# Loads, matmuls and top-k rounds put in another order at the start of a one-core hybrid decoder step

## What is computed

```python
def index_topk(iq, iw, ik, q_pos, topk):
    s = jax.nn.relu(jnp.einsum('bqhd,bld->bqhl', iq, ik))
    score = jnp.einsum('bqhl,bqh->bql', s, iw).astype(jnp.float32)
    ...
    score = jnp.where(causal, score, -jnp.inf)
    _, idx = lax.top_k(score, topk)
...
    p = rmsnorm(x, norm_mix_g) @ w_in
    a_q, a_k, a_v, i_q, i_k, i_w, p_b, c_q, gates = split_last(p, IN_SIZES)
    a_q = rope_partial(a_q.reshape(B, T, N_HEADS_A, HEAD_DIM_A), pos, ROT_A)
...
    ik_past = cache_idx_k[page_table].reshape(DB, PAST_LEN, IDX_DIM)
```

## Time and profile before

| | |
|---|---|
| median of three runs | 1349.66 us (1349.17 to 1350.88) |
| the profiled execution | 1349.81 us, its span from the first to the last instruction 1347.9 us |
| PE busy | 1234.8 us, 92% of the span |
| DVE busy | 710.7 us, 53% |
| ACT busy | 407.2 us, 30% |
| the p loop's first matmul | at 156.79 us |
| the decode attention's first matmul (L1126) | at 283.42 us |
| mean granted clock of PE | 0.970 |

### The profile page before, as it was taken

One profiled execution on the slowest core, in us unless ns is written; L12 is line 12 of the kernel. 1 busy time (PEld: TensorE's weight loads), 2 busy tenths in 40 slices (PEclk: granted clock), 3 DMA queues, 4 the chain that ended last, 5 costly groups with the idle time before them and its releaser, 6 DMA issues.

```text
span 1347.9 us, 25134 instructions
## 1 busy us (share of the span) xinstructions
PE 1234.8 (92%) x10585; PEld 1094.1 (81%) x10589; DVE 710.7 (53%) x1126; ACT 407.2 (30%) x791; POOL 86.3 (6%) x140
## 2 busy tenths in 40 slices
PE   6699699889969988998998999999999999999995
PEld 4476476658657777887887889999999999999994
DVE  5499798714043284365346337755544434434445
ACT  2110144424322423343234234233333123123120
POOL 0100100002102042002001002000000000000000
PEclk9899799999989999999999999999999999999997
DMA  7113143513500022022013215562122312223211
GB/s 305 31 28 156 35 167 120 178 35 156 200 0 10 33 79 89 18 97 97 18 56 118 73 43 161 170 235 95 63 94 74 114 63 95 95 67 121 77 50 67
DMA packets 39218, 127.52 MB, mean 95 GB/s; under 512 B 5203, under 2 KB 17491, under 8 KB 29635
## 3 DMA queue, kind: packets, MB, share of 16 engines
q1 hardware_dynamic: 37666, 121.36, 25.3%
q0 software_dynamic: 1440, 4.56, 1.0%
HBM read 111.77 MB, written 14.13 MB: 93 GB/s over the span
## 4 chain that ended last, share of the span: by engine, by line
PE 78%; DVE 15%; ACT 2%; issue 2%; DMA 1%; POOL 1%; SPq 0%; DVEq 0%; ACTq 0%; POOLq 0%
PE ps L923 13%; PE ps L924 12%; PE ps L927 12%; PE ps L951 8%; PE ps L1281 4%; PE ps L960 3%; PE ps L961 3%; PE ps L962 3%; PE ps L904 2%; DVE R L1999 2%; DVE small L1998 2%; PE ps L1233 2%; PE ps L946 1%; PE ps L949 1%; DVE wl L558 1%
## 5 line engine op out<-in xcount | busy, mean ns | idle before, releaser
L548 ACT ACTIVATE wh<-land 128x1024 fp32r<-128x1024 f32 (+1 forms) x120 | 116.2, 970 | 185.6 <-PE ps L927 185.6
L951 PE MATMUL ps<-xn,ring 128*128 128x272 f32 x576 | 149.4, 403 | 9.4 <-ACT pb L1593 9.4
L558 DVE TENSOR_TENSOR wl<-land,wh 128x1024 fp32r<-128x1024 f32 (+1 forms) x120 | 136.0, 1136 | 27.7 <-ACT wh L548 26.9
L923 PE MATMUL ps<-xhi,wh 128*128 128x272 f32 x512 | 138.9, 289 | 2.3 <-DVE wl L558 1.2
L923 PE MATMUL ps<-hh,wh 128*128 128x272 f32 x512 | 138.8, 288 | 0.0
L924 PE MATMUL ps<-hl,wh 128*128 128x272 f32 x512 | 138.3, 288 | 0.0
L924 PE MATMUL ps<-xlo,wh 128*128 128x272 f32 x512 | 138.3, 288 | 0.0
L951 PEld LDWEIGHTS ps<-xn,ring 128*128 128x128 f32 x576 | 105.4, 192 | 34.6 <-ACT pb L1593 9.8
L960 PE MATMUL ps<-xhi,wh 128*128 128x272 f32 x384 | 124.2, 324 | 4.2 <-issue 3.6
L961 PE MATMUL ps<-xlo,wh 128*128 128x272 f32 x384 | 113.3, 295 | 0.0
L962 PE MATMUL ps<-xhi,wl 128*128 128x272 f32 x384 | 113.2, 295 | 0.0
(11 more groups left out here) (407 smaller groups left out, 2368.8 us busy)
## 6 DMA issues: line engine op xcount, KB each, us to landing
land<-in_slabs SPq DMA_DIRECT2D x48, 1024.0 KB, 4.8
ring<-in_slabs SPq DMA_DIRECT2D x17, 1024.0 KB, 8.1
gates<-R SPq DMA_DIRECT2D x24, 272.0 KB, 2.0
merge<-gates SPq DMA_DIRECT2D x24, 272.0 KB, 4.1
land<-in_slabs SPq DMA_DIRECT2D x12, 512.0 KB, 3.9
xT<-in_mks SPq DMA_DIRECT2D x8, 512.0 KB, 4.9
R<-in_kv SPq DMA_DIRECT2D x24, 128.0 KB, 2.0
pb<-in_kv SPq DMA_DIRECT2D x24, 128.0 KB, 2.0
```

The costliest lines, as they stand in the source:

```text
L548: act.activation(hi, src, ACT.Copy).then_inc(s["weights_hi"], 1)
L558: eng.tensor_tensor(lo, src, hi.bitcast(F32), ALU.subtract).then_inc(s["weights_lo"], 1)
L923: pe.matmul(ps[:, b + h, 0:HALF], whi[:, k], hi[k][:, c], start=a, stop=False)
L951: mm = pe.matmul(ps[:, b, 0:HALF], W[:, k, c0_:c0_ + w], xn3[:, k, cols], start=a, stop=z)
```

## The change

It touches the kernel up to the decode attention, on every engine.

- **Loads**: the small vectors and the first quarter of x first, then slab 0, the other quarters of x, the constants, slab 1. The order from there on is as before; the key page row `kv_row(0)` is issued after `kv_row(1)`, since its place in SBUF (the start of `xT`) now holds scores of block 3.
- **Head weights**: `iw` had 4 columns. It now has 32, and job 1 puts four of its eight k tiles in each accumulation, each into 32 output partitions of its own (L1007 of the changed kernel). A matmul with the constant `sel` adds the four groups (L1029), in place of a transpose.
- **Prompt scores**: block 3 gets a buffer of its own (`rl3`), and the three blocks are computed early, with pieces of jobs 4 and 5 between them.
- **DVE**: blocks 1 and 2 first, with the rotations of two `aq` tiles after block 1; then the heads' weighing of the decode scores, the norm of the memory and the copies; block 3 last, with the other rotations between its rounds.
- **PE**: jobs 4 to 6, then the decode scores and the memory's norm, then jobs 7 to 9.
- **Fill steps**: 24 steps (three `mk` jobs) go ahead of the p loop (`("pre", 0)`), and from u = 13 on a group has 3 steps in place of 4.
- The memory's norm sums go to PSUM bank 7. The semaphores are renamed: `padded` for `zi_set` and `za_set`, `tables` for `consts` and `bias_done`, `selected` counts `ss_out` too.

```diff
-    s = [("w_in", 0, KT, [(IK, 64), (IK, 64), (IK + 64, 4)]), ("w_in", 0, KT, [(IQ, 256)])]
+    s = [("w_in", 0, KT, [(IK, 64), (IK, 64), (IK + 64, 32)]), ("w_in", 0, KT, [(IQ, 256)])]
...
-    waits = [(("p", u), 5 if u < 13 else 4) for u in range(36)]
+    waits = [(("pre", 0), 24)]
+    waits += [(("p", u), 5 if u < 13 else 3) for u in range(36)]
...
-        rl = cut(R, B + 5312, 4, 512)
+        rl, rl3 = cut(R, B + 5312, 4, 512), cut(xT, 0, 4, 512)
...
-            sp.dma_start(cst[:, 0:first], i["const"][:, 0:first]).then_inc(s["ones_in"], 16)
-            for n in range(2):
-                sp.dma_start(xT3[:, 4 * n:4 * n + 4], i["xT"][:, 4 * n:4 * n + 4]).then_inc(s[f"x_in{n}"], 16)
-            sp.dma_start(vec[:, :], i["vec"]).then_inc(s["ones_in"], 16)
+            sp.dma_start(vec[:, :], i["vec"]).then_inc(s["vec_in"], 16)
...
+            x_pair(0)
...
-            stream(0, 2)
+            stream(0, 1)
+            for n in range(1, 4):
+                x_pair(n)
+            sp.dma_start(cst[:, 0:first], i["const"][:, 0:first]).then_inc(s["ones_in"], 16)
+            stream(1, 2)
...
             sp.wait_ge(s["norm_out"], 8)
-            kv_row(0)
             kv_row(1)
             sp.wait_ge(s["isum"], 12)
+            kv_row(0)
             kv_row(2)
...
+            slab_wait(pe, JOBS[1][2])
+            W, b = slab(0), bank_of(1)
+            for h in range(2):
+                for k in range(KT):
+                    g = slice(32 * (k % 4), 32 * (k % 4) + 32)
+                    mm = pe.matmul(ps[g, b + h, 0:HALF], W[:, k, P:P + 32], xg3[:, k, h * HALF:(h + 1) * HALF],
+                                   start=(k < 4), stop=(k >= 4))
+            mm.then_inc(s["gemm_done"], 1)
...
+            rope(4)
+            part(6, xn3, 2, KT)
+
+            pe.wait_ge(s["padded"], 5)
+            pe.wait_ge(s["rope_sin"], 5)
             for q in range(2):
                 pe.wait_ge(s[f"ki_in{q}"], 128 * 4)
-            pe.wait_ge(s["relu"], 12)
             for b in range(DB):
...
+            norm(1, NMEM)
             pe.wait_ge(s["selected"], 1)
...
-            pe.wait_ge(s["ss_out"], 1)
-            for n in range(3, 8):
-                rope(n)
-
-            pe.wait_ge(s["rope_sin"], 8)
+            part(7, xn3, 0, KT)
+            pe.wait_ge(s["selected"], 2)
+            pe.wait_ge(s["norm_rt"], 2)
+            rope(5)
+            part(8, xn3, 0, 2)
+            rope(6)
+            part(8, xn3, 2, KT)
+            part(9, xn3, 0, 2)
+            rope(7)
+            part(9, xn3, 2, KT)
...
+            pe.wait_ge(s["norm_out"], 16)
+            fill("pre", 0)
...
+            for t in range(1, 3):
+                row_scores(t)
                 for _ in range(TOPK_P // 8):
-                    take_eight(sc, m8)
...
+                    take_eight(scp[:, 0:P * (t + 1)], m8)
+                row_bias(t)
+                if t == 1:
+                    rope(3)
+                    rope(4)
...
             dve.wait_ge(s["ki_used"], 8)
             dve.tensor_scalar(rs, flat, 0.0, iws, ALU.max, ALU.mult).then_inc(s["selected"], 1)
+            norm(1, memT, memn, NMEM, "norm_mem_g")
             dve.wait_ge(s["i_rows"], 2)
...
+            row_scores(3)
+            for n in range(TOPK_P // 8):
+                if n in (6, 10):
+                    rope(5 if n == 6 else 6)
+                take_eight(scp, m8)
+            row_bias(3)
+            rope(7)
```

More of the change, by code:

```diff
@@ L992, in _, with part, prompt_scores @@
                 job(0, xg3, only=k)
-            pe.wait_ge(s["ones_in"], 32)
+            pe.wait_ge(s["ones_in"], 16)
             norm_sum(0)
[L995 to L1001, removed]
-                rope(n)
[L1003 to L1011, removed]
+            slab_wait(pe, JOBS[1][2])
[6 more added lines that the diff above has]
+            mm.then_inc(s["gemm_done"], 1)
+            def part(n, src, first, last):
+                for k in range(first, last):
+                    job(n, src, only=k)
+            def prompt_scores(t):
                 for h in range(4):
@@ L1017, in _ @@
                               start=True, stop=True).then_inc(s["iscore"], 1)
[L1018 to L1022, removed]
+            job(2, xg3)
+            part(3, xg3, 0, 3)
+            pe.wait_ge(s["inputs_in"], 16)
+            out_of(1, pe)
+            for t in range(5):
+                w = P if t < 4 else NS
+                mm = pe.matmul(ps[0:w, 7, 4 * t:4 * t + 4], iwT[:, P * t:P * t + w], k_("sel")[:, 0:4], start=True, stop=True)
+            mm.then_inc(s["i_rows"], 1)
+            rope(0)
+            part(3, xg3, 3, 6)
+            pe.wait_ge(s["padded"], 1)
+            rope(1)
+            part(3, xg3, 6, KT)
+            rope(2)
+            pe.wait_ge(s["rope_out"], 3)
+            prompt_scores(1)
+            part(4, xn3, 0, 2)
+            prompt_scores(2)
+            part(4, xn3, 2, 5)
+            prompt_scores(3)
+            part(4, xn3, 5, KT)
+            part(5, xn3, 0, 5)
+            pe.wait_ge(s["relu"], 12)
+            rope(3)
+            part(5, xn3, 5, KT)
+            part(6, xn3, 0, 2)
+            rope(4)
+            part(6, xn3, 2, KT)
+            pe.wait_ge(s["padded"], 5)
+            pe.wait_ge(s["rope_sin"], 5)
             for q in range(2):
                 pe.wait_ge(s[f"ki_in{q}"], 128 * 4)
-            pe.wait_ge(s["relu"], 12)
             for b in range(DB):
@@ L1551, in norm @@
                 else:
-                    act.activation(nbuf[n][1][:, 0:N], ps[:, 4, 0:N], ACT.Sqrt, bias=epsc, scale=1.0 / D).then_inc(s["norm_rt"], 1)
+                    act.activation(nbuf[n][1][:, 0:N], ps[:, 7, 0:N], ACT.Sqrt, bias=epsc, scale=1.0 / D).then_inc(s["norm_rt"], 1)
             def evac(n):
@@ L1617, in _ @@
             act.wait_ge(s["pool_step"], 2)
+            act.activation(small[:, 142:143], epsc, ACT.Square)
             norm(0, xT3, TOK)
-            act.wait_ge(s["aux_in"], 48)
-            norm(1, memT, NMEM)
-            act.wait_ge(s["norm_out"], 16)
+            act.wait_ge(s["norm_out"], 8)
             for t in range(1, 4):
@@ L1989, in _ @@
                 else:
[L1990 to L1991 removed]
+                    ins.then_inc(s["padded"], 1)
+            dve.tensor_copy(biasp[:, 0, 0:P], k_("caus")).then_inc(s["tables"], 1)
+            rope(0)
+            rope(1)
+            take(3, iq[:, 1])
+            rope(2)
+            dve.wait_ge(s["padded"], 1)
             flat = ps[:, 4:7].rearrange("p a b -> p (a b)")[:, 0:KEYS]
[L1994 removed]
             def take_eight(sc, m8):
@@ L2001, in _, with row_scores @@
             m8 = small[:, 132:140]
-            for t in range(1, 4):
+            def row_scores(t):
                 n = P * (t + 1)
-                sc = scp[:, 0:n]
+                sc, rows = scp[:, 0:n], rl if t < 3 else rl3
                 for h in range(4):
```

113 lines of the change are left out of this document (55 added, 58 removed).

## The result

The change takes 1365.97 us (median of four runs, 1364.68 to 1367.01) against 1349.41 us (1347.54 to 1350.88) for the kernel before: 1.28% slower, ratio 1.0128 with an interval of 1.0109 to 1.0146. Forecast were 1350.3 us, 1346 to 1356. The profiled execution spans 1363.9 us against 1347.9.

What follows compares the result with a forecast made beforehand. It took SP's page reads, then DVE's list, to set the p loop's start: 164.5 + 126.6 - 7.1 = 284.0 us for the decode attention against 283.42, 0.6 us later, so 1350.3 us, range 1346 to 1356.

Steps and rivals of the forecast that it cites:

- What bounds the kernel, and the cover: Front: SP's page reads, 1.25 us each, gate the decode scores, so earlier loads, head weights and prompt scores gain nothing.
- When the pages are there: SP's queue: larger slab 0 adds 0.3 us, last page lands at 101.7 us, PE starts at about 101.8 us.
- The decode scores: On PE after the pause: 15.7 us plus 2.35 us for 4.7 us at half clock, ending at 119.85 us.
- Rival 2: Decode scores on PE: 64-row matmuls don't raise the clock, all run at half, 13.4 us more, 1363.7 us; chance 0.09.
- DVE's list: DVE between decode scores and p loop: norm, copies, block 3, rotations, 44.6 us; p loop starts at 164.5 us.
- PE's own list: PE between decode scores and p loop: norm, sum, jobs, rotations, transposes, fill steps, some 43.5 us, just shorter than DVE's.
- The p loop: Loop before decode attention: fill steps moved ahead shorten it by 7.1 us from 126.6; starting at full clock counted as 0.
- Rivals 3 and 4: P loop: second groups give nothing, 3.7 us more, 1354.0 us, chance 0.13; all steps come back, 1346.6 us, chance 0.12.
- Rival 1: Front: pages don't gate the decode scores, DVE is the limit, 1328 us taken; chance 0.06.

Runs made afterwards that it cites:

- early: The changed kernel with page numbers loaded first on ACT's queue, SP waiting only for them and the small vectors: 1356.70 us.
- before_early: The kernel before the change, with page numbers loaded first on ACT's queue: 1350.02 us against 1349.37, ratio 1.0009.
- rows128: The changed kernel with the decode scores' 24 matmuls on all 128 rows, zero weights in half of them: 1354.55 us.
- pages64: The changed kernel, 64-row scores kept, with page numbers loaded first, 16 pages issued by ACT, and the memory's norm ahead of the scores: 1328.86 us.
- packed: The changed kernel with two batches of decode scores in each 128-row matmul, 12 matmuls in place of 24: 1343.36 us, ratio 0.9958.
- warm76: The changed kernel with 76 filling matmuls of 128 rows ahead of PE's wait for the pages: 1357.76 us.
- warm50: The changed kernel with 50 filling matmuls of 128 rows ahead of PE's wait for the pages: 1366.38 us.
- warm128: The changed kernel with 60 filling matmuls of 128 rows ahead of PE's wait for the pages: 1351.56 us profiled, 1366.63 to 1367.03 in four others.
- best: The changed kernel with page numbers first, 16 pages issued by ACT, memory's norm ahead of the scores, and 12 decode-score matmuls of 128 rows: 1330.24 us.

## Why the prediction was wrong, step by step

- *What bounds the kernel, and the cover.* Right. SP's pages were the gate (early, before_early), and padding, earlier x and the scores in a row were hidden under them: PE idled 28 us, DVE 39 us.
- *When the pages are there.* 101.8 us forecast, 104.05 measured. I added 0.3 us for the larger slab and took the rest of SP's queue as it was; in fact, with the loads reordered, SP's first page read came 1.4 us later and each page cost 0.02 us more, 1.1 us over 63 pages; why a page cost more no run shows.
- *The decode scores.* This step failed. I took 4.7 us at half clock from two rises, one behind matmuls of 128 rows and one behind pairs on both halves, and applied them to matmuls of 64 rows. The clock did come back in 4.9 us for 128 rows (rows128), and not at all in 30.85 us for 64 on one half. The price is 12.8 us in the scores, and 1.2 us more on DVE's list, which waits for the norm behind them (6.45 us on PE in place of 4.64).
- *Rival 2* described just this, at 1363.7 us (13.4 us over the forecast), with a chance of 0.09. Its evidence against, that the same matmuls had held 1.00 before, was no evidence: pages64 shows that the 64-row scores held a clock that was up, and the change, against rows128, that they did not bring it up. To hold and to raise are two questions, and the trace of before answered the first only. With both rises resting on other shapes, the rival should have had a chance near the forecast's own, and the range should have reached it.
- *DVE's list.* 44.6 us forecast; 45.85 in the change, 44.2 in packed, where the norm ran at full clock. Right. (The terms of PE's own list add up to 43.8 us, not 43.5; DVE was the later all the same, by 0.59 us.)
- *The p loop.* 7.1 us forecast, 7.2 measured, with the waits of 1.2 and 1.7 us that were named. The split was off: 5.6 us from steps, 1.6 from the clock, which I had set off against the wider steps at 0. That the sum came out is in part luck.
- *Rivals 3 and 4.* Neither: the second groups show no wait of their own, and the waits of the first groups did grow. *Rival 1*, pages that don't gate, was priced at 1328 us; pages64, where they don't and the norm goes ahead as well, takes 1328.86 us; with that second edit in it, it is no test of the price.

The Trainium skill (TensorE: Matmul & The Clock Gate, section The HAM clock gate (the "warmup" mystery)) has the clock follow how busy PE has been of late. By that rule alone the scores, with PE busy for 30.95 of 31 us, would have come back to 1.00 as those of rows128 did; the change's trace disagrees, at 0.50 throughout. Its section HAM oscillation — how this bites in real kernels has waits for DMA pull the clock down, and the trace agrees: 28.09 us of waiting for pages, and 0.50 behind it.

## What to carry to other kernels

When a reorder lets an engine come early to work that a transfer still holds back, the pause is not free: ask what runs first behind it, and on how many rows. Matmuls on the same 64 rows did not bring the clock back here, so fill the pause up to them with work on 128 rows (warm76, 8 us under the change, though its filling is of no use), or pack two into one of 128 rows, which halves their number as well (packed, 23 us under). And look at what starts the transfer: here a wait for loads that it did not need held the scores back by 12 us.

## What the runs showed of the hardware that was not expected

- 24 matmuls on the lower 64 rows (16 of 512 columns, 8 of 32) kept PE busy for 30.8 us at 0.50 without a rise, after 28.09 us of pause and after 14.36 us (early); the same columns on 128 rows had 1.00 after 4.9 us, with zero weights in half of the rows. Matmuls of 64 rows that went by turns to both halves had it after 6.1 us (kernel before, 65.2 to 71.3 us). Without a pause ahead, 64 rows held 1.00 for 15.7 us (pages64).
- A pause of 2.77 us was enough, and the clock fell 2.1 us after it had ended, under 64-row matmuls in progress (warm50). By my reading such pauses make a kernel's time depend on when a DMA lands: warm128 took 1351.56 us once and 1367 us four times.
- ACT reads a page number and issues its DMA about as fast as SP: 16 pages in 18.66 us (best), where SP takes 1.27 us a page. PE did not wait for them.
